# Routed experts in 32-row tiles: four column strips, rings for the token rows, up products one tile ahead of the down products

## The reference

```python
scores = sigmoid(h @ router_w)                 # (512, 16)
# biased scores choose one group of 4 experts, then 2 experts inside it; w = normalised scores
for e in range(16):
    he = silu(h @ w1[e]) * (h @ w3[e])         # w1, w3: 1024 x 512
    out = out + gate[:, e:e + 1] * (he @ w2[e])    # w2: 512 x 1024
```

## Time and profile before

| | us |
|---|---|
| median of 3 runs (lowest, highest) | 1958.69 (1956.73, 1961.2) |
| the profiled execution | 1965.64 |
| its span, first to last instruction | 1964.0 |
| tile loop, first `up` to the end of the last `down` | 1590.41 to 1923.80 |
| TensorE busy over the span | 1720.4 (88%) |
| mean granted TensorE clock | 0.949 of full speed |

### The profile page before, as it was taken

The page is one execution under the profiler, slowest core; times in us unless marked ns, Lnnn a source line. Parts: engine busy times, 40 slices in busy tenths (PEclk is TensorE's granted clock), DMA queues, the critical chain, the costliest instruction groups (busy, mean ns, idle before and its releaser), DMA issues.

```text
span 1964.0 us, 17655 instructions
## 1 busy us (share of the span) xinstructions
PE 1720.4 (88%) x6784; PEld 945.7 (48%) x6785; DVE 736.4 (37%) x1229; ACT 380.6 (19%) x651; POOL 266.8 (14%) x272
## 2 busy tenths in 40 slices
PE   4988899799789879999999999999999569999791
PEld 0553454355355344544545555446564236666460
DVE  1144644653754554600027774123143312222124
ACT  2321232132132121000123334101100201111111
POOL 0003412421430540000000000000000021111014
PEclk9999989899989889999999999999999879999896
DMA  9611101011021025621120111215205749887974
GB/s 315 253 40 43 43 22 43 4 61 43 1 86 43 0 78 217 219 85 45 49 79 0 43 44 43 86 44 184 86 0 215 264 155 372 308 297 257 379 268 141
DMA packets 108941, 243.50 MB, mean 124 GB/s; under 512 B 7913, under 2 KB 17134, under 8 KB 108882
## 3 DMA queue, kind: packets, MB, share of 16 engines
q1 hardware_dynamic: 86800, 180.59, 26.0%
q0 software_dynamic: 14128, 50.60, 7.4%
q10 hardware_dynamic: 7954, 11.50, 1.6%
HBM read 220.40 MB, written 22.28 MB: 124 GB/s over the span
## 4 chain that ended last, share of the span: by engine, by line
PE 74%; DVE 13%; ACT 4%; issue 3%; POOL 2%; DMA 2%; ACTq 1%; SPq 1%; DVEq 0%; POOLq 0%; PEldq 0%
PE psum L419 15%; PE psum L998 9%; PE psum L431 8%; PE psum L709 6%; PE psum L1023 4%; PE psum L596 4%; PE psum L423 4%; PE psum L824 3%; PE psum L654 2%; PE psum L622 2%; PE psum L493 2%; PE psum L441 2%; PE psum L858 1%; PE psum L756 1%; DVE arena L1621 1%
## 5 line engine op out<-in xcount | busy, mean ns | idle before, releaser
L419 PE MATMUL psum<-arena 128*128 128x512 f32 x688 | 315.2, 615 | 9.7 <-issue 4.0
L419 PEld LDWEIGHTS psum<-arena 128*128 128x128 f32 x688 | 133.3, 197 | 171.9 <-issue 164.1
L998 PE MATMUL psum<-arena 128*64 128x256 f32 x1664 | 190.5, 387 | 10.8 <-DMA arena<-exp_w_d 9.2
L998 PEld LDWEIGHTS psum<-arena 128*64 128x64 f32 x1664 | 144.7, 139 | 62.6 <-issue 29.0
L431 PE MATMUL psum<-arena 128*128 128x512 f32 x352 | 151.6, 592 | 0.0
L596 PE MATMUL psum<-arena 128*128 128x512 f32 x256 | 130.7, 641 | 1.2 <-ACT arena L1172 1.2
L709 PE MATMUL psum<-arena 128*128 128x512 f32 x256 | 111.6, 593 | 0.0
L431 PEld LDWEIGHTS psum<-arena 128*128 128x128 f32 x352 | 66.8, 190 | 83.3 <-issue 83.2
L1023 PE MATMUL psum<-arena 128*64 128x512 f32 x416 | 95.0, 596 | 6.1 <-ACT arena L1439 6.1
L2013 POOL TENSOR_TENSOR arena<-arena 128x512 f32<-128x512 f32 x40 | 49.5, 1247 | 359.4 <-ACT arena L1227 309.2
L2049 POOL TENSOR_TENSOR arena<-arena 128x512 f32<-128x512 f32 x64 | 82.6, 1294 | 103.0 <-ACT arena L1267 103.0
(11 more groups left out here) (340 smaller groups left out, 2096.6 us busy)
## 6 DMA issues: line engine op xcount, KB each, us to landing
arena<-exp_w_d SPq DMA_DIRECT2D x48, 2048.0 KB, 19.1
arena<-w_in_d SPq DMA_DIRECT2D x22, 2048.0 KB, 7.8
arena<-ada_w_d POOLq DMA_DIRECT2D x8, 2048.0 KB, 9.1
slots<-arena POOLq DMA_DIRECT2D x1, 8704.0 KB, 26.3
arena<-ada_w_d SPq DMA_DIRECT2D x4, 2048.0 KB, 23.4
arena<-ssd_proj_d SPq DMA_DIRECT2D x4, 2048.0 KB, 9.8
arena<-slots POOLq DMA_DIRECT2D x28, 256.0 KB, 6.4
slots<-arena POOLq DMA_DIRECT2D x54, 128.0 KB, 5.3
```

The lines of the kernel that those rows point to most:

```text
L419: ins = mmul(ps[:, 0:T], slot[:, k, m * P:(m + 1) * P], src[:, k, C:NT], start=(k == 0), stop=(k == KD - 1))
L998: ins = mmul(ps[q * R:(q + 1) * R, 0:HF], XT[:, k, :], w[:, k, q * HF:(q + 1) * HF], start=(k == 0), stop=(k == KD - 1))
```

## The change

- A tile has 32 rows. Every expert gets at least two tiles: two, plus one for each multiple of 32 above 32 that its count exceeds. With the counts above: 3, 2, 3, 2, 5, 3, 3, 5, 2, 2, 2, 2, 2, 3, 3, 2 tiles, 44 in all.
- Output columns are cut in four: four strips of 32 PSUM partitions (q = 0 to 3), each with a stationary operand of 128 x 32. w1 and w3 share one product: its 256 moving columns are 128 of w1 and 128 of w3. `up` is 32 products of 256 columns, `down` 16 products of 256 columns.
- Rows lie in quarters: a tile is 128 partitions x 256 values (quarter q of row r on partition 32q + r). Its transposition is two 128 x 128 pieces, that of `hg` one. `xrow` and `ysb` are rings of four tiles. POOL loads and stores in batches of two tiles, one DMA of 128 KB for each tile and direction, made of 1 KB pieces. ACT copies a tile out of the ring into `xq` before PE transposes it.
- PE's order becomes: transpose of `hg` of tile j - 1, up of tile j, transposes of the rows of tile j + 1, down of tile j - 1. At an expert's begin the wait for its weights stands ahead of the whole group, so ahead of the last down of the expert before.

```diff
-ROWS_A_TILE = 64
-HF = FF // 2
-XTILES = 2 * T // ROWS_A_TILE + NE + 2
+ROWS_A_TILE = 32
+NQ = P // ROWS_A_TILE
+HF = FF // NQ
+DQ = D // NQ
+BATCH = 2
+RING = 2 * BATCH
+XTILES = 2 * T // ROWS_A_TILE + 2 * NE + 4 * BATCH
...
-        xrow = alloc(D)
+        xrow = alloc(RING * DQ)
...
+        xq = alloc(DQ)
-        heT = alloc(HF // P, P)
-        ysb = alloc(D // 2)
+        heT = alloc(NQ, ROWS_A_TILE)
+        ysb = alloc(RING * DQ)
...
+        w13 = [view(off, (2, KD, FF)) for off in (wset0, 0, phase_base)]
...
+            def turn_x():
+                for i in range(DQ // P):
+                    ins = nc.tensor.transpose(psX[:, i * P:(i + 1) * P], xq[:, i * P:(i + 1) * P], ident)
+                ins.then_inc(S_("x_turned"), 1)
 
             def up(p, j):
 
                 pe.wait_ge(S_("x_ready"), j + 1)
                 pe.sem_inc(S_("pe_passed"), 1)
-                for i, (ps, name) in enumerate(((psG, "g_full"), (psU, "u_full"))):
-                    w = wmem[p][i].rearrange("p (k n) -> p k n", k=KD)
-                    for k in range(KD):
-                        for q in range(2):
-                            ins = mmul(ps[q * R:(q + 1) * R, 0:HF], XT[:, k, :], w[:, k, q * HF:(q + 1) * HF],
-                                       start=(k == 0), stop=(k == KD - 1))
-                    ins.then_inc(S_(name), 1)
...
+                for k in range(KD):
+                    for q in range(NQ):
+                        ins = mmul(psU[q * R:(q + 1) * R, 0:2 * HF], XT[:, k % 2, k // 2, :],
+                                   w13[p][:, :, k, q * HF:(q + 1) * HF], start=(k == 0), stop=(k == KD - 1))
+                ins.then_inc(S_("u_full"), 1)
+                pe.wait_ge(S_("xq_ready"), j + 2)
                 pe.sem_inc(S_("pe_passed"), 1)
-                turn_x(0, KD - 3)
+                turn_x()
+
+            def turn_h(j):
+
                 pe.wait_ge(S_("he_ready"), j + 1)
                 pe.sem_inc(S_("pe_passed"), 1)
-                for i in range(HF // P):
-                    ins = nc.tensor.transpose(psH[:, i * P:(i + 1) * P], hg[:, i * P:(i + 1) * P], ident)
-                ins.then_inc(S_("h_turned"), 1)
-                turn_x(KD - 3, KD)
+                nc.tensor.transpose(psH[:, 0:P], hg, ident).then_inc(S_("h_turned"), 1)
 
             def down(p, j):
...
-                for k in range(FF // P):
-                    for q in range(2):
-                        ins = mmul(psD[q * R:(q + 1) * R, :], heT[:, k % 2, k // 2 * R:(k // 2 + 1) * R],
-                                   w2[:, k, q * 512:(q + 1) * 512], start=(k == 0), stop=(k == FF // P - 1))
+                for k in range(NQ):
+                    for q in range(NQ):
+                        ins = mmul(psD[q * R:(q + 1) * R, 0:DQ], heT[:, k, :],
+                                   w2[:, k, q * DQ:(q + 1) * DQ], start=(k == 0), stop=(k == NQ - 1))
                 ins.then_inc(S_("down_full"), 1)
 
+            def tile(p, j, p_before):
+
+                turn_h(j - 1)
+                up(p, j)
+                down(p_before, j - 1)
...
+            def expert(e, p, p_before, arrived):
+
+                lo = bound(e, 2)
+                hi = bound(e + 1, 4)
                 pe.wait_ge(S_("w_in%d" % p), arrived)
                 pe.sem_inc(S_("pe_passed"), 1)
...
+                tile(p, lo, p_before)
+                with pe.Fori(lo + 1, hi) as j:
+                    tile(p, j, p)
...
+            def x_row(j):
+
+                act.wait_ge(S_("xrow_in"), (j // BATCH) * (16 * BATCH) + 16 * BATCH)
+                run(xq, xrow[:, bass.ds((j & (RING - 1)) * DQ, DQ)], ACT.Copy).then_inc(S_("xq_ready"), 1)
...
+            with act.Fori(1, n) as j:
+                hidden(j - 1)
+                gate(j)
+                act.wait_ge(S_("x_turned"), j + 2)
+                x_row(j + 2)
...
-            step(v.tensor_scalar(ntile, ntile, 1.0, None, ALU.add))
+            step(v.tensor_scalar(ntile, ntile, 2.0, None, ALU.add))
...
+            with dve.Fori(1, n) as j:
+                hidden(j)
                 modulate_x(j + 2)
+                out_rows(j)
+            out_rows(n)
...
+            nb = (n + (BATCH - 1)) // BATCH
+            with pool.Fori(0, nb - 1) as b:
+                pool.wait_ge(S_("xq_ready"), b * BATCH + BATCH)
+                pool.wait_ge(S_("xrow_in"), b * (16 * BATCH) + 2 * 16 * BATCH)
+                load_x(b + 2)
+                pool.wait_ge(S_("y_ready"), b * BATCH + BATCH + 1)
+                pool.wait_ge(S_("y_sent"), b * (16 * BATCH) + 2 * 16 * BATCH)
+                send_y(b)
```

More of the change, by code:

```diff
@@ L269, in build @@
         cnt = alloc(NE)
-        over = alloc(NE, T // ROWS_A_TILE - 1)
+        over = alloc(NE, T // ROWS_A_TILE - 2)
         ntile = alloc(NE)
@@ L1025, in down, with bound @@
                 ins.then_inc(S_("down_full"), 1)
[L1027 to L1031, removed]
+            def tile(p, j, p_before):
+                turn_h(j - 1)
+                up(p, j)
+                down(p_before, j - 1)
+            def bound(e, least):
+                at = first_tile_i[0:1, e:e + 1] if isinstance(e, int) else first_tile_i[0:1, bass.ds(e, 1)]
+                return pe.value_load(at, min_val=least, max_val=XTILES)
@@ L1032, in expert @@
+            def expert(e, p, p_before, arrived):
+                lo = bound(e, 2)
+                hi = bound(e + 1, 4)
                 pe.wait_ge(S_("w_in%d" % p), arrived)
                 pe.sem_inc(S_("pe_passed"), 1)
[L1034 to L1040, removed]
-            pe.wait_ge(S_("tiles_known"), 1)
-            with pe.Fori(0, NE // NW) as trio:
-                for p in range(NW):
-                    expert(trio * NW + p, p, trio * 48 + 48)
@@ L1045, in _ @@
-            expert(NE - 1, 0, NE // NW * 48 + 48)
+                tile(p, lo, p_before)
+                with pe.Fori(lo + 1, hi) as j:
+                    tile(p, j, p)
+            pe.wait_ge(S_("xq_ready"), 1)
+            turn_x()
+            pe.wait_ge(S_("tiles_known"), 1)
+            hi = bound(1, 2)
+            pe.wait_ge(S_("w_in0"), 48)
+            up(0, 0)
+            with pe.Fori(1, hi) as j:
+                tile(0, j, 0)
+            with pe.Fori(0, NE // NW) as trio:
+                for i in range(NW):
+                    p = (i + 1) % NW
+                    expert(trio * NW + i + 1, p, i, trio * 48 + (96 if p == 0 else 48))
@@ L1048, in _ @@
+            n = bound(NE, 2 * NE)
+            turn_h(n - 1)
+            down(0, n - 1)
         @block.sync
@@ L1851, in _ @@
                     dve.wait_ge(*is_full((name, j)))
-                    dst, half = g1row[:, j * 512:(j + 1) * 512], slice(0, P)
-                    if name == "g2":
-                        half = slice(j * 64, (j + 1) * 64)
-                        dst = g2half[half, :]
-                    v.tensor_copy(dst, bank((name, j))[half, :]).then_inc(is_free((name, j))[0], 1)
+                    if name == "g1":
+                        ins = v.tensor_copy(g1row[:, j * 512:(j + 1) * 512], bank((name, j)))
+                    else:
+                        for q in range(2):
+                            rows = slice((2 * j + q) * ROWS_A_TILE, (2 * j + q + 1) * ROWS_A_TILE)
+                            ins = v.tensor_copy(g2q[rows, :], bank((name, j))[rows, q * DQ:(q + 1) * DQ])
+                    ins.then_inc(is_free((name, j))[0], 1)
             for j in range(2):
@@ L1929, in _ @@
                                      ALU.add))
[L1930 to L1931 removed]
+            more = T // ROWS_A_TILE - 2
+            step(v.tensor_tensor(over, before[:, TL, :].unsqueeze(2).to_broadcast([P, NE, more]),
+                                 r_("filled_tiles")[:, 1:].unsqueeze(1).to_broadcast([P, NE, more]), ALU.is_gt))
             step(v.tensor_reduce(ntile, over, AX.X, ALU.add))
[L1933 removed]
+            step(v.tensor_scalar(ntile, ntile, 2.0, None, ALU.add))
             step(v.memset(first_tile, 0.0))
@@ new lines, in _, with load_x, send_y @@
+            part = lambda ring, tile: ring[:, bass.ds((tile & (RING - 1)) * DQ, DQ)]
+            def load_x(b):
+                for i in range(BATCH):
+                    pool.dma_start(part(xrow, b * BATCH + i), quarters(b * BATCH + i)).then_inc(S_("xrow_in"), 16)
+            def send_y(b):
+                for i in range(BATCH):
+                    pool.dma_start(quarters(b * BATCH + i), part(ysb, b * BATCH + i)).then_inc(S_("y_sent"), 16)
+            load_x(0)
+            pool.wait_ge(S_("y_ready"), 1)
@@ new lines, in _ @@
+            for i in range(RING):
+                if i == BATCH:
+                    pool.wait_ge(S_("y_sent"), 16 * BATCH)
+                pool.dma_start(slots[(XTILES - 1 - i) * R:(XTILES - i) * R, :].rearrange("r (q c) -> q r c", q=NQ),
+                               ysb[:, i * DQ:(i + 1) * DQ]).then_inc(S_("y_sent"), 16)
+            pool.wait_ge(S_("xrow_in"), 16 * BATCH)
+            load_x(1)
```

(1 more changed line is left out.)

85 lines of the change are left out of this document (39 added, 46 removed).

## The result

The changed kernel took 1939.52 us (median of 4 runs, 1939.05 to 1940.62) where the kernel before took 1958.97 beside it (1956.73 to 1961.20). The ratio is 0.990, with an interval of 0.9885 to 0.9916. So it is faster, by 19.4 us, and that is half of the 39 us that were forecast. The profiled execution took 1939.05 us, its span 1937.4.

What follows compares the result with a forecast made beforehand. The loop was taken as PE-bound, DMA close behind, with weight loads setting the late beat: 292.4 + 0.3 + 1.5 makes 294 us, 39 under 333.4; 1958.69 less 39 is 1919.7, say 1919.5 us; range 1907 to 1943.

Steps and rivals of the forecast that it cites:

- The beat of PE: Tile loop on PE: four strips at a pitch of 0.054 us, 6.2 us a tile against 12.21 for twice the rows.
- rival 2: PE's up and down: a floor on instructions, pitch 0.062, tile 7.0, loop 321 us, a gain of 12; chance 0.06.
- rival 3: PE's up and down: four strips no faster than two, pitch 0.108, 180 us longer (2138); chance 0.07 in full.
- The waits at the late experts: End of the loop: PE waits for the weights' DMA at experts 12 to 15 and hardly before.
- The weights: SP's weight reloads: 6.2 us a matrix, 18.6 an expert, despite 1 KB row pieces; upper bound 7.2 a matrix.
- The recursion: Whole loop: each expert begins when its weights are there and the expert before is done; ends at 292.4 us.
- rival 1: Tile loop: heavier beat or heavier DMA, still faster; gain 22 (tile 6.6, matrix 6.5) or 15 (6.2, 7.2); chance 0.15.
- theory F: Row DMAs, stated for the experiments: a slowest dimension of 4 uses few of 16 engines, and the weights wait for those.
- An expert's begin: PE's sequencer between experts: 0.3 us charged for each of 15 begins, 4.5 in all; bounds 0 and 1.8.
- The ring of rows: POOL's row loads and stores: 8.5 us needed of 10 available, so it fits, with one more tile of time behind.
- one of the text's own signs of being wrong: Profile of the changed kernel: waits for the rows' ring would make the prediction wrong.
- the low clock: PE at 1.2 GHz: an expert's first tile is 3 us longer after a stall of over 3 us, and at the start.

Runs made afterwards that it cites:

- experiment 7: Changed kernel with row loads spread (slowest dimension 128 instead of 4) and result stores spread (32 instead of 4), still 1 KB pieces: 1917.97 us, ratio 0.978.
- experiment 4: Kernel before with row loads and result stores cut into 1 KB pieces, slowest dimension still large, same bytes: 1957.44 us, ratio 0.999.
- experiment 5: Changed kernel with the row loads alone spread, slowest dimension 128 instead of 4, same 1 KB pieces: 1927.68 us, ratio 0.982.
- experiment 8: Kernel before with row loads and result stores reordered to a slowest dimension of 4 instead of 64, same pieces and bytes: 2007.12 us, ratio 1.023.
- experiment 6: Changed kernel with the result stores alone spread, four DMAs a batch, slowest dimension 32 instead of 4: 1934.86 us, ratio 0.987.
- experiment 10: Changed kernel with row loads and stores both spread, and reloads moving only half of each weight matrix (computation incomplete): 1910.72 us, ratio 0.975.
- experiment 3: Changed kernel with the reloads for experts 3 to 15 moving only the first half of each weight matrix: 1918.80 us, ratio 0.979.

## Why the prediction was half right

**The beat of PE: right.** Up took 3.59 us for 64 instructions in the chain, a pitch of 0.056 (forecast 0.054, 3.46), down 1.86 for 32 with its filling (1.73 and 0.19), the tile 6.08 to 6.09 (6.2). Four strips run side by side at almost four times the rate of one, so rivals 2 and 3 fall. The Trainium skill, page "TensorE: Matmul & The Clock Gate", section "Wait — 56ns, not 53.3ns?", could have spoken for a floor of about 62 ns; the 56 ns of this trace don't show one there. 44 tiles, and the SiLU and the product beside PE (0.289 us for the product), came as forecast. The waits at the late experts came earlier and larger: 17.3 us from expert 11 on, the longest (7.00) at expert 11, where the text has them at experts 12 to 15.

**The weights: the step that failed.** The text says of the row DMAs "their pieces become 1 KB", bounds a matrix by 6.2 and 7.2 us, and then "I take 6.2, as SP's big pieces are unchanged". From the first packet at 1603 us to the last at 1876 the 39 matrices took 7.0 us each, and 7.2 in the stretch of the earlier trace rows. The recursion has the first load begin later, 22 us into the loop (1608); counted from there it is 6.87. That was close to the upper bound, and rival 1's case, which I had given 0.15. With tile and begin as measured the recursion gives 292.9 us at 6.2 and 304.3 at 6.87, so this one term is 11.4 of the 14.8. Experiment 7, whose row DMAs are spread, has a loop of 292.6. The reason taken was beside the point: what SP's own pieces look like says nothing on what other transfers leave it. What I priced, size, costs nothing (experiment 4); what I didn't look at, the order of the dimensions in `quarters`, costs it (experiments 5, 7, 8), by the loads and not by the stores (experiments 5 and 6). The diff shows it, `rearrange("r (q c) -> q r c", q=NQ)`.

The trace doesn't say on which of the 16 engines a DMA runs. It shows that such DMAs land later, 8.6 us for 128 KB, and slow a queue that has nothing to do with them. The Trainium skill, page "DMA: Bandwidth & Descriptors", sections "Why a DMA increments its semaphore by 16 and not by 1" and "Rules for kernel authors", has the rule: the number of engines that share a DMA is set by its slowest dimension, so one of 4 is left with 4 of 16. The runs agree with that in sign; the cost to others, 35 to 62 GB/s of the weights, it doesn't give. I cited the same page for 512 B and missed this rule. Why the large transfers lose as much as this (theory F has them wait for the busiest engine) is argued and not shown.

**An expert's begin: half of its size.** 0.3 us was charged inside bounds of 0 and 1.8; experiment 10 has 0.67 in the mean: ten begins with 0.50, all of which goes with one count read, and five with 1.0. The text had the pieces (1.8 us of sequencer before the first product, 1.9 of down) and took the difference of two numbers read from different places. In after the list has 6.8 / 11 = 0.62, much the same. Only with half weights and rows in quarters is it 1.04 (experiment 3). There the count read itself is slower, in its longest case four times; the reads of experiments 3 and 10 from 1600 to 1890 us, ns shortest, median and longest:

```profile
L1033 PEldq TENSOR_LOAD <-arena x31: 294/322/1285, 1600.2 to 1868.5; - x31
```

```profile
L1033 PEldq TENSOR_LOAD <-arena x31: 297/306/348, 1600.3 to 1860.9; - x31
```

What holds these reads up is open.

Tile and begin together explain only 0.5 of the loop's 14.8, since a quicker tile (0.1 x 44) pays for the begins, and where weights are late the begins don't count.

**The ring of rows: it didn't always fit.** The text needed 8.5 us of 10, with 6.4 to land. As measured that is 4 x 0.69 of issue and 8.6 to land, an estimate of 11.4. The tile of slack that the text had behind it hid this but once: at 1776.49 PE waited 3.14 us for a row, one of the text's own signs of being wrong, and that beat took 11.0 us instead of 6.08. PE then waited 7.00 us more for expert 11's weights, so it isn't shown that the late row made the loop longer. With the loads or the stores spread (experiments 5 and 6) PE waits for rows 0.3 and 1.0 us, with both 0.

**The end: not forecast.** Behind the loop 2.6 us more pass, 2.2 of them in the last store of results, 4.73 us where it was 2.50. It has the same slow form; spread, it takes 1.93.

**What is left.** With all measured terms the recursion and its edges give 305.8 of 308.8. Most of the 3.0 us between lies behind the last begin. Redone with these terms, the recursion has expert 15 begin 291.2 us into the loop, and it began at 291.6; but from there to the end 17.1 us passed, where two tiles and the end alone give 14.4. Of these 2.7, 1.7 are the `up` of 5.35 us behind the stall of 1.95. The recursion charges the low clock only behind stalls of over 3 us, a limit that stands in no row: here a stall of 1.95 brought it, and in experiment 6 one of 2.13 didn't (3.67 us). What it charges, 3 us, is too much for these tiles too: behind the stalls of 7.00, 4.37, 3.52 and 1.95 us in after `up` took 5.35 to 6.38 us instead of 3.66. In numbers, 294 forecast, + 11.4 weights, + 0.5 tile and begin, + 1.7 low clock at the end, + about 1.2 open = 308.8. And the program: 24.6 of loop less 2.6 behind it is 22.0, where the medians show 19.4; the profiled execution of before was 7 us above its own median, after's at its own, and 2.6 us lie well within the scatter of the part ahead of the loop (starts from 1580.9 to 1595.5).

**Range and chances.** 1939.5 lay inside 1907 to 1943, and "faster" was right, but the loop of 308.8 is outside the 282 to 304 that had the chance of 0.66, and the gain is half of the one forecast. The range held since the bound of 7.2 had been carried into it; the chance of 0.15 for it was too small, for an operation of which no row existed in this form.

## What to carry to other kernels

Read a DMA's two access patterns for the slowest dimension before pricing its bytes or pieces: put a large one there (32, 64 and 128 did well here, 4 didn't), and let the engine that reads the tile undo the order in an access pattern that it has anyway. When a loop is near the DMA limit, price every change of a small transfer at what it does to the big ones, and keep the pessimistic bound as a case in full where no row shows the new form. When work is cut finer, count each sequencer's steps per outer iteration against the work that hides them: a begin's reads were free behind a down of 3.65 us, and behind one of 1.86 one of them cost 0.48 us.

## What the runs showed of the hardware

- Four column strips of float32 products start one 256-column instruction each 0.056 us, where one strip needs 0.226 and two 0.108. The weight loads, as many as the products, stay hidden.
- 128 KB row DMAs with a slowest dimension of 4 land in 8.6 us beside full queues, in 6.0 us with one of 128 (experiment 5), and in 5.3 us when the stores are spread too; the same 256 KB load goes from 6.4 to 12.6 us by a change of order alone.
- Such DMAs leave many packets under 512 B in the record: 2294 from 1620 to 1680 us in after, 611 in experiment 7. Half weights make it plain, with equal bytes in both. From 1600 to 1860 us of experiment 3, and then of 10:

```profile
q1 hardware_dynamic: 17264, 40.90, 49.9%
q0 software_dynamic: 11520, 10.61, 16.0%
```

```profile
q1 hardware_dynamic: 17264, 40.90, 45.6%
q0 software_dynamic: 4544, 10.62, 13.3%
```

  The rows' queue has 11,520 packets against 4,544, and the weights' packets, the same ones, take 49.9% of the engines' time against 45.6%. What the small packets are, the record doesn't say.
- POOL's issue of one such DMA takes longer too: 0.69 to 0.70 us, against 0.53 before and 0.55 to 0.57 in experiment 7. The slowest dimension is not alone in it: in experiment 4, 1 KB pieces with one of 64 cost 0.63. From POOL's order of time in after:

```profile
1647.08 0.69 POOL L2138 DMA_DIRECT2D arena<-slots  x1 [0.67 <-issue]
```
